# Moving small jobs of ScalarE, VectorE and TensorE by one weight chunk, and writing a loop of merge rounds out

## The reference

```python
# first block
mem_n = rms_norm(mem, norm_mem_g);  h = rms_norm(x, norm_in_g)
proj = h @ w_in                      # qa, ka, va, za, qb, kb, vb, zb, qm, zm, gates
ya = moba_attention(rope(qa), rope(ka), va) * silu(za)      # 8 heads of 128, causal here
yb = dilated_mixture(rope(qb), rope(kb), vb) * silu(zb)     # 3 groups of 4 heads
ym = memory_attention(qm, mk, mv) * silu(zm)                # mk, mv = mem_n @ w_mem_kv
merged = g_a * (ya @ w_proj_a) + g_b * (yb @ w_proj_b) + g_m * (ym @ w_proj_m)
x = rms_norm(x + merged @ w_out)
# second block
u = rmsnorm(x);  proj = u @ w_in_2   # lru_x, lru_g, q, k, v, ret_g
y = concat(rg_lru(conv(lru_x)) * gelu(lru_g), retention(rope(q), rope(k), v) * silu(ret_g))
h = x + y @ w_out_2
u = rmsnorm(h);  h = h + (silu(u @ w_gate) * (u @ w_up)) @ w_down
out = rmsnorm(h)
```

## Time and profile before

| | |
|---|---|
| runs | 2203.16, 2203.64, 2203.76 us (median 2203.64) |
| profiled execution: span | 2202.4 us |
| profiled execution's own time | not recorded apart; its span and what lies around it |
| granted TensorE clock | full speed, 0.99 and more in every slice |
| TensorE busy | 2185.7 us, 99% |
| VectorE busy | 1308.7 us, 59% |
| ScalarE busy | 1025.3 us, 47% |
| weight loads, SP's queue | 408.7 MB, 59.9% of the 16 DMA engines |
| carries, POOL's queue | 53.5 MB, 8.0% |

### The profile page before, as it was taken

One profiled execution on the slowest core, in us unless ns is written; L12 is line 12 of the kernel. 1 busy time (PEld: TensorE's weight loads), 2 busy tenths in 40 slices (PEclk: granted clock), 3 DMA queues, 4 the chain that ended last, 5 costly groups with the idle time before them and its releaser, 6 DMA issues.

```text
span 2202.4 us, 26200 instructions
## 1 busy us (share of the span) xinstructions
PE 2185.7 (99%) x9906; PEld 1811.4 (82%) x9906; DVE 1308.7 (59%) x1646; ACT 1025.3 (47%) x1235; POOL 144.2 (7%) x242
## 2 busy tenths in 40 slices
PE   9999999999999999999999999999999999999998
PEld 7888888887888888888888888888888888888886
DVE  5655656666455645546676878665555555554454
ACT  5544444443444444444554666454444444444443
POOL 0010101011000000000111100110001000100000
PEclk9999999999999999999999999999999999999999
DMA  8775656567754657667778756586777777776664
GB/s 293 219 230 177 203 164 214 182 225 220 219 163 148 211 177 229 201 204 282 228 259 249 229 182 200 192 247 210 211 211 225 220 211 211 227 236 193 194 194 146
DMA packets 228673, 464.65 MB, mean 211 GB/s; under 512 B 16344, under 2 KB 16608, under 8 KB 227680
## 3 DMA queue, kind: packets, MB, share of 16 engines
q1 hardware_dynamic: 212128, 408.73, 59.9%
q0 software_dynamic: 15712, 53.49, 8.0%
q10 hardware_dynamic: 736, 1.12, 0.1%
HBM read 437.59 MB, written 25.69 MB: 210 GB/s over the span
## 4 chain that ended last, share of the span: by engine, by line
PE 90%; DVE 4%; DMA 3%; ACT 1%; issue 1%; POOL 0%; POOLq 0%; ACTq 0%; DVEq 0%
PE ps L1485 29%; PE ps L1487 29%; PE ps L1486 29%; DVE w_lo L861 1%; DMA stage<-bounce 1%; PE ps L1345 1%; ACT w_hi L575 1%; PE ps L1376 1%; PE ps L1398 1%; DMA bounce<-tmp 1%; DVE tmp L1023 1%; DVE tmp L1014 0%; DVE stage L1009 0%; DVE stage L1018 0%; DMA raw<-in_w_out 0%
## 5 line engine op out<-in xcount | busy, mean ns | idle before, releaser
L861 DVE TENSOR_TENSOR w_lo<-raw,w_hi 128x1024 fp32r<-128x1024 f32 (+1 forms) x776 | 931.5, 1211 | 766.8 <-ACT w_hi L575 764.9
L575 ACT ACTIVATE w_hi<-raw 128x1024 fp32r<-128x1024 f32 (+1 forms) x776 | 810.3, 1050 | 917.2 <-PE ps L1487 824.5
L1485 PE MATMUL ps<-w_hi,xT_hi 128*128 128x512 f32 x1088 | 430.2, 395 | 1.6 <-DVE w_lo L861 1.6
L1487 PE MATMUL ps<-w_hi,xT_lo 128*128 128x512 f32 x1088 | 424.2, 390 | 0.0
L1486 PE MATMUL ps<-w_lo,xT_hi 128*128 128x512 f32 x1088 | 423.6, 389 | 0.0
L1485 PE MATMUL ps<-w_hi,u2T_hi 128*128 128x512 f32 x704 | 274.0, 389 | 0.0
L1487 PE MATMUL ps<-w_hi,u2T_lo 128*128 128x512 f32 x704 | 273.9, 389 | 0.0
L1486 PE MATMUL ps<-w_lo,u2T_hi 128*128 128x512 f32 x704 | 273.9, 389 | 0.0
L1485 PEld LDWEIGHTS ps<-w_hi,xT_hi 128*128 128x128 f32 x1088 | 204.4, 188 | 44.1 <-DVE w_lo L861 3.3
L1487 PEld LDWEIGHTS ps<-w_hi,xT_lo 128*128 128x128 f32 x1088 | 204.2, 188 | 43.5
L1486 PEld LDWEIGHTS ps<-w_lo,xT_hi 128*128 128x128 f32 x1088 | 204.5, 188 | 40.7
(11 more groups left out here) (262 smaller groups left out, 2259.3 us busy)
## 6 DMA issues: line engine op xcount, KB each, us to landing
raw<-in_w_in SPq DMA_DIRECT2D x368, 512.0 KB, 4.5
raw<-in_w_ffn_gate SPq DMA_DIRECT2D x88, 512.0 KB, 4.3
raw<-in_w_ffn_up SPq DMA_DIRECT2D x88, 512.0 KB, 4.5
raw<-in_w_ffn_down SPq DMA_DIRECT2D x88, 512.0 KB, 4.0
raw<-in_w_out SPq DMA_DIRECT2D x64, 512.0 KB, 5.1
bounce<-tmp POOLq DMA_DIRECT2D x41, 512.0 KB, 3.3
stage<-bounce POOLq DMA_DIRECT2D x164, 128.0 KB, 5.3
raw<-in_w_mem_kv SPq DMA_DIRECT2D x32, 512.0 KB, 5.7
```

What stands on the lines that cost most here:

```text
L575: nc.scalar.activation(w_hi[:, s, 0:per], raw[:, s, 0:per], ACT.Copy).then_inc(hi_ready, 1)
L861: nc.vector.tensor_tensor(w_lo[:, s, 0:per], raw[:, s, 0:per], w_hi[:, s, 0:per].bitcast(F32), ALU.subtract)\
L1485: nc.tensor.matmul(bank(2 * par + t), x_hi, w_hi[:, s, k], start=first, stop=False)
L1487: ins = nc.tensor.matmul(bank(2 * par + t), x_lo, w_hi[:, s, k], start=False, stop=last)
```

## The change

Six edits, all of order:

1. Mem's squares: two Squares behind split 6 become one behind split 6 and one behind split 7; VectorE's `mem_factors` goes from behind split 7 to behind split 1 of the next tile.
2. Units 5, 6 and 9, 10, 11 get `y_late`: TensorE turns y after chunk 6 instead of 5, and `unit_hi` and `unit_lo` go from the end of the tile to behind split 1 of the next one.
3. The six rotary blocks of qb and kb are marked "late", so that `use_late` stands behind split 3 where it stood behind split 1. For qb nothing changes, since blocks posted in a unit's tile are already late.
4. The residual's `post` on VectorE goes from behind split 3 to behind split 4 in w_out's tiles, ScalarE's `post_job` for bounced residuals from 4 to 5.
5. `ret_decay(4)` goes from chunk 4 to chunk 3 of the tail.
6. `w.rounds` for the merge rounds is replaced by a Python loop on SP, ScalarE, VectorE and TensorE: the same work in straight code.

```diff
@@ -334,13 +334,15 @@
                         dict(w=w_in, col=c + 3072, x="x", post=("silu", za[half][:, :, :]))]
                 for n in range(4):
                     four[n]["unit"] = mem_unit(n) if half == 0 else moba_unit(n)
+                    four[n]["y_late"] = half == 1 and n in (1, 2)
                 out_ += four
-            ten = [dict(w=w_in, col=QB + NW * g, x="x", post=("rope", qbT, g * QUAD)) for g in range(3)]
-            ten += [dict(w=w_in, col=KB + NW * g, x="x", post=("rope", kbT, g * QUAD)) for g in range(3)]
+            ten = [dict(w=w_in, col=QB + NW * g, x="x", post=("rope", qbT, g * QUAD, "late")) for g in range(3)]
+            ten += [dict(w=w_in, col=KB + NW * g, x="x", post=("rope", kbT, g * QUAD, "late")) for g in range(3)]
             ten += [dict(w=w_in, col=VB + NW * g, x="x", post=("take", vb[:, g])) for g in range(3)]
             ten += [dict(w=w_in, col=ZB, x="x", post=("silu", zb[:, :, :]))]
             for n in range(4):
                 ten[n]["unit"] = moba_unit(QUAD + n)
+                ten[n]["y_late"] = n > 0
             return out_ + ten
 
         def tiles_merge(n, first=False):
@@ -473,7 +475,8 @@
             load(second, {h: lambda h=h: load_x(h // QUAD, h % QUAD) for h in range(NT * QUAD)})
             sp.dma_start(consts[:, C_ID + P:], consts_d[:, C_ID + P:]).then_inc(in_tables, 16)
             load_all(rest + tiles_attention() + tiles_merge(0))
-            w.rounds(sp, NG - 1, lambda i: load_all(tiles_merge(i + 1)))
+            for i in range(NG - 1):
+                load_all(tiles_merge(i + 1))
             w.rounds(sp, NG // 2, lambda i: load_all(res_tiles(w_out, "m", None, i)))
             load_all(tiles_two())
             load_all(tiles_out2())
@@ -575,14 +578,18 @@
                 nc.scalar.activation(w_hi[:, s, 0:per], raw[:, s, 0:per], ACT.Copy).then_inc(hi_ready, 1)
                 w.step("g")
 
+            def square(src, sums, t):
+
+                if w.n["sq"]:
+                    act.wait_ge(sq_done, w.n["sq"])
+                nc.scalar.activation(sq_out[:, 0:D], src[:, t], ACT.Square, accum_out=sums[:, t:t + 1]).then_inc(sq_done, 1)
+                w.step("sq")
+
             def squares(src, sums, ready):
 
                 for t in range(NT):
                     ready(t)
-                    if w.n["sq"]:
-                        act.wait_ge(sq_done, w.n["sq"])
-                    nc.scalar.activation(sq_out[:, 0:D], src[:, t], ACT.Square, accum_out=sums[:, t:t + 1]).then_inc(sq_done, 1)
-                    w.step("sq")
+                    square(src, sums, t)
 
             def tile_squares(prev):
 
@@ -733,6 +740,8 @@
                 unit = tile.get("unit")
                 for h, _ in enumerate(chunks(tile)):
                     split(tile)
+                    if prev and prev.get("y_late") and h == 1:
+                        unit_hi(prev["unit"])
                     if h == late_in(tile, late):
                         use_late()
                     if "lru" in tile and h == 1:
@@ -749,11 +758,11 @@
                         lru_tanh(tile["lru"])
                     if "lru" in tile and h == 6:
                         lru_sqrt(tile["lru"])
-                    if h == pos(tile, 7 if unit else 4 if prev and prev["post"][0] == "res" and bounced(prev["post"]) else 6):
+                    if h == pos(tile, 7 if unit else 5 if prev and prev["post"][0] == "res" and bounced(prev["post"]) else 6):
                         post_job(prev, bool(unit))
                     for f in dict(hooks).get(h, ()):
                         f()
-                if unit and unit_chunk(tile, h) == 7:
+                if unit and unit_chunk(tile, h) == 7 and not tile.get("y_late"):
                     unit_hi(unit)
                 if "lru" in tile:
                     lru_hi(tile["lru"])
@@ -779,7 +788,7 @@
 
             four = tiles_memkv()
             four[0]["act_hooks"] = {1: jobs(memT_hi, V_MEM, 1), 3: jobs(memT_hi, V_MEM, 2), 5: jobs(memT_hi, V_MEM, 3),
-                                    6: [mem_in, lambda: squares(mem_tok, sumsq_m, lambda t: None)]}
+                                    6: [mem_in, lambda: square(mem_tok, sumsq_m, 0)], 7: [lambda: square(mem_tok, sumsq_m, 1)]}
             four[1]["act_hooks"] = {7: [lambda: act.wait_ge(b_out, 16),
                                         lambda: squares(x_tok, sumsq_x, lambda t: act.wait_ge(in_x[t], 16 * QUAD))]}
             for n in (2, 3):
@@ -810,7 +819,8 @@
             tiles[0]["act_hooks"] = {1: last}
             prev = chain(tiles, prev)
             prev = chain(tiles_merge(0, first=True), prev)
-            w.rounds(act, NG - 1, lambda i: chain(tiles_merge(i + 1), merge_last(i)))
+            for i in range(NG - 1):
+                chain(tiles_merge(i + 1), merge_last(i))
             prev = merge_last(NG - 1, "end")
             for k in range(NG // 2):
                 prev = chain(res_tiles(w_out, "m", x1, k, what="u"), prev)
@@ -1157,6 +1167,8 @@
                 unit = tile.get("unit")
                 for h, _ in enumerate(chunks(tile)):
                     split(tile)
+                    if prev and prev.get("y_late") and h == 1:
+                        unit_lo(prev["unit"])
                     if h == late_in(tile, late):
                         use_late()
                     if "lru" in tile and h == 2:
@@ -1165,7 +1177,7 @@
                         ret_lo(prev["ret"])
                     if unit and unit_chunk(tile, h) == 4:
                         unit_mask(unit)
-                    if h == pos(tile, 5 if unit else 3):
+                    if h == pos(tile, 5 if unit else 4 if prev and prev["post"][0] == "res" and bounced(prev["post"]) and prev["post"][3] == "u" else 3):
                         post(prev, h + 1)
                     if "ret" in tile and h == 4:
                         ret_decay(tile["ret"])
@@ -1177,7 +1189,8 @@
                         f()
                 if unit and unit_chunk(tile, h) == 7:
                     unit_norm(unit)
-                    unit_lo(unit)
+                    if not tile.get("y_late"):
+                        unit_lo(unit)
                 if "lru" in tile:
                     lru_scan(tile["lru"])
                 if "ret" in tile:
@@ -1275,7 +1288,8 @@
                 w.step("j0", "h0")
 
             four[0]["dve_hooks"] = {0: [second_half], 1: jobs(memT_hi, memT_lo, V_MEM, 1), 3: jobs(memT_hi, memT_lo, V_MEM, 2),
-                                    5: jobs(memT_hi, memT_lo, V_MEM, 3), 7: [mem_factors]}
+                                    5: jobs(memT_hi, memT_lo, V_MEM, 3)}
+            four[1]["dve_hooks"] = {1: [mem_factors]}
             for n in (2, 3):
                 four[n]["dve_hooks"] = {6: jobs(xT_hi, xT_lo, V_IN, 2 * n - 4), 7: jobs(xT_hi, xT_lo, V_IN, 2 * n - 3)}
             last = four[3]["dve_hooks"].pop(7)
@@ -1287,7 +1301,8 @@
             tiles[0]["dve_hooks"] = {1: last}
             prev = chain(tiles, prev)
             prev = chain(tiles_merge(0, first=True), prev)
-            w.rounds(dve, NG - 1, lambda i: chain(tiles_merge(i + 1), merge_last(i)))
+            for i in range(NG - 1):
+                chain(tiles_merge(i + 1), merge_last(i))
             prev = merge_last(NG - 1, "end")
             for k in range(NG // 2):
                 tiles = res_tiles(w_out, "m", x1, k, what="u")
@@ -1302,7 +1317,7 @@
             first_half = dict(tiles[4])
             tiles[6]["dve_hooks"] = {1: [lambda: turn_rows(h2, slice(0, NW))], 3: [lambda: post_job(first_half, False)]}
             tail_hooks(tiles[:6], "dve_hooks", {
-                4: [lambda: ret_decay(4)], 5: [lambda: ret_norm(4)],
+                3: [lambda: ret_decay(4)], 5: [lambda: ret_norm(4)],
                 7: [lambda: ret_decay(5), lambda: ret_lo(4)], 8: [lambda: ret_norm(5)],
                 10: [lambda: ret_decay(6), lambda: ret_lo(5)], 11: [lambda: ret_norm(6)],
                 13: [lambda: ret_decay(7), lambda: ret_lo(6)], 14: [lambda: ret_norm(7), lambda: ret_lo(7), lambda: dve.wait_ge(in_h2, 16 * NT * NG)],
@@ -1466,7 +1481,7 @@
                 unit, need, hooks = tile.get("unit"), tile.get("need", {}), tile.get("pe_hooks", {})
                 if w.n[f"a{par}"]:
                     pe.wait_ge(acc_free[par], w(f"a{par}"))
-                at_ = (0, 2, 4, 5)
+                at_ = (0, 2, 4, 6 if tile.get("y_late") else 5)
                 by_rows = SLOTS if tile.get("by_rows") else 0
                 for i, h in enumerate(chunks(tile)[:hcs - by_rows]):
                     s = w.n["g"] % SLOTS
@@ -1578,7 +1593,8 @@
             for k, units in ((3, 4), (4, 12), (5, 16)):
                 tiles[k]["need"] = {0: [lambda units=units: pe.wait_ge(u_lo, units)]}
             prev = chain(tiles, prev)
-            w.rounds(pe, NG - 1, lambda i: chain(tiles_merge(i + 1), merge_last(i)))
+            for i in range(NG - 1):
+                chain(tiles_merge(i + 1), merge_last(i))
```

## The result

| | before | changed |
|---|---|---|
| median of 9 runs, us | 2203.16 | 2207.91 |
| lowest to highest, us | 2201.0 to 2204.03 | 2205.89 to 2211.07 |
| span of the profiled execution, us | 2202.4 | 2205.0 |
| that execution's own time, us | not recorded apart | 2206.8 |

The ratio is 1.0021, 95% interval 1.0013 to 1.0030: by the medians the change costs 4.75 us. Forecast were 2202.8 and a range up to 2206.4, so the result lies outside it, on the side of the slower rival. All ratios in this document leave out two executions far above the others at a lower clock, one of e6 (4124 us) and one of the kernel before that was run beside e5 to e8 (3149 us).

The account below looks back on a forecast made before the run. TensorE, almost always busy, was taken as the bound, with only its stalls winnable. Gains of 4.8 and 1.05 against 5 d at d = 1.0 netted 0.8 us: 2202.8 us from the median, range 2198.2 to 2206.4.

Parts of the forecast that it names:

- the slower rival: Turns of units 7, 10, 11 and chunk 164: carries slowed by 2.1 us each, time 2208.2 us; chance 0.08.
- The five small edits: Squares, rotary copies, merge rounds, residual posts and retention's decay: gains of 4.77 us together from removed TensorE stalls.
- the squares: Mem's squares, stall at chunk 7: gain 0.69 us, or nothing if chunk 8 then stalls instead.
- the two rotary places: Chunk 4 after a rotary carry: moving the copy behind split 3 gains 0.64 + 1.06 = 1.70 us.
- the rounds: First chunks of the looped merge rounds: written out, they gain 0.12 + 0.40 + 0.11 = 0.63 us.
- the residual: Stall at 1092.17: the post behind chunk 4's w_lo gains 0.94 us; a later carry may return up to 0.9.
- the retention: Stall at 1386.09: decay one chunk earlier gains 0.81 us, or nothing if the scores it reads were late.
- The ends of the units: Five y stalls, 2.05 us, go with y later; waits at unit 7's turn and chunk 164 leave 1.05 net.
- The loop: Units' closed chain of turn, transpose, bounce, stage, copy, split, mask, exp: limits units once y does not; carry delays add up.
- d: Slowing of each stage carry 7 to 11 by earlier weight loads: 1.0 us, bounds 0.2 and 2.1, counted five times.
- the rival: Merge rounds: writing them out does nothing, VectorE being late for another reason; 0.6 missing, 2203.4 us; no separate chance given.
- The rule of turns between the queues: Stage carries: DMA engines alternate queues by packet, so a load 1.9 us sooner takes half; estimated d 0.9, sum -1.3.

Follow-up runs that it names:

- e6: Changed kernel with the loads of chunk 4 held until yT_lo is written and the rotary copy behind the exp in units' tiles; 2198.45 us, ratio 0.9980.
- e5: Changed kernel without y_late and with the rotary copy behind the exp in units' tiles; 2200.84 us, ratio 0.9988.
- e8: Changed kernel with y_late on units 6 and 10 alone, which are not neighbours; 2203.21 us, ratio 1.0001.
- e3: Changed kernel, but SP holds the load of chunk 4 behind each y_late unit until VectorE has written its yT_lo; 2197.28 us, ratio 0.9968.
- e4: Changed kernel with the rotary carry's copy behind the exp in units' tiles, not ahead of split 4; 2199.91 us, ratio 0.9982.
- e7: Changed kernel with only the load of chunk 5 behind each y_late unit held until yT_lo is written, chunk 4's left early; 2205.59 us, ratio 1.0009.
- e9: Changed kernel with the load of chunk 4 behind each y_late unit waiting for one w_lo more; 2203.09 us, ratio 1.0001.
- e2: Kernel before the change with y_late alone added; 2214.18 us, ratio 1.0052.
- e1: Changed kernel with y_late taken out and the other five edits kept; 2198.65 us, ratio 0.9982.

## Why the prediction was wrong

**The five small edits**: right in sign and place, all of them, and the sum a little too small: 4.77 by the brackets, and 5.5 came. By the offsets between the passes of both kernels the squares gave 0.9 (0.69 forecast), the two rotary places 0.5 and 1.4 (0.64 and 1.06), the rounds 0.7 (0.63), the residual 1.1 (0.94) and the retention 0.9 (0.81). At the squares and the second rotary place some 0.15 of it comes a few passes behind the stall, which the bracket does not show. Nothing came back at chunk 5 of the residual tiles.

**The ends of the units**: the y stalls went, as said, and the turns of units 7, 10 and 11 and chunk 164 took their place, as said; that of unit 6 too, which I had not named. The loop was right, e3 and e4 break it at two links. That its delays add up from unit to unit is shown only in part, by e8. The y stalls gave back 3.0 us where I had 2.05.

**The step that failed is the size of d.** I read 7.2 us now and 8.3 with the first load 0.6 us behind, put between two single carries, and rounded to 1.0. Measured is 8.80 - 7.13 = 1.67, and over all profiled executions with the first load about 2.5 or 0.5 us behind, e6 and e7 left out, some 2.2 (6.85 and 9.10). The row at 1.6 us (7.4) on which the interpolation hung is one carry, and e9's five at 1.7 average 7.8, from 7.0 to 8.6; a single carry's spread was as large as the effect. With 1.67, -5.8 + 5 x 1.67 = +2.5, close to the 2.6 by which the profiled span grew, though by luck, since two errors cancel: 0.9 us more gained outside the units (0.2 of it at the start, by no edit), and 1.0 more lost in them (8.3 against 7.3).

**The step that was missing is the clock.** I priced a stall at its own length. The one at turn 7 grew to 3.4 us, since the carry's slip met the smallest slack, and 1.6 us of slow passes came on top, in the changed kernel, in e2 and in e7. (I had worked out the slip per carry and never the length of the single stall.)

**The range** reached to d = 1.7 and so held the 1.67 of this profile by a hair. What it did not hold is the step from the profile to the median: I took the median at 1.2 us above the span, as before, and it lies 2.9 above it (2207.91 and 2205.0). Without these 1.7 us the result would stand at 2206.2, inside the range, with the cost of each carry wrong all the same. Part of this is that the changed kernel's runs spread over 5 us and the profiled one is a quick one. Why they spread more than the 3 us of before was not tried by itself; e9 spreads 9 us with as little slack, e1 3 us, and part of any spread can be the start, where the profiled executions alone differ by 3 us.

**The rivals.** The slower one was the right mechanism in the right places, at a chance of 0.08, which was too low: its threshold, d of 1.9, left out the clock. Its time, 2208.2, was all but met, yet with a d of 1.67 and not 2.1, so by luck. The rounds did bring all of 0.63, so the rival falls: the entry and the exit of the loop, which the rule on taken branches (Trainium skill, Runtime: NRT & Kernel Launch, "Instruction fetch mechanics") leaves as they are, went from 0.39 and 0.38 to 0.27 too, so the rule would explain 0.40 of it and the trace shows the rest; no run parts the branch from the loop's register work. The rule of turns between the queues (Trainium skill, DMA: Bandwidth & Descriptors, "Queues, rings and completion order") gave 0.9 by an even split, an estimate; the profile after has 1.67 for 2 us, e7 1.5, and e9 0.7 for 0.8 us. The sign agrees, the size is well over the even split; why was not tried.

## What to carry to other kernels

A job that is moved away from a queue's head lets through what stood behind it, and that may be a release of a buffer and with it a DMA: before moving it, look at which transfer will start sooner and what is in flight then. Here the move cost 8 us, and one wait on the queue that issues the loads took that away; e3, the changed kernel with that wait, is 0.9968 [0.9956, 0.9981] of before and beats both. Most of this gain is that of the five other edits: without `y_late` at all (e1) it is 0.9982 [0.9973, 0.9991], and the two intervals overlap, so that the late y is a gain by itself, 1.4 us by the medians and 2.4 by the profiles, is likely and not shown. Where a closed loop of engines and DMAs runs beside the bounding engine with 0.3 us of slack, price anything that touches its transfers by several of them, not by one.

## What the runs showed that I had not expected

- A load that starts 0.5 us behind the first of the four stage DMAs lengthens their landing by 1.5 us alone, and the second by only 0.2 more, less than the spread (e7). The four are issued over 2.4 us, and a load that starts behind the last costs little (e3).
- Nominally equal carries differ much: before, with the first load 2.5 us behind in four of five, they took 6.55 to 7.85 us. A cost of 1 us can't be read from one of them.
- A stall of 3.40 and of 3.35 us (changed kernel, e2) was followed by some 3.6 us at 1.2 GHz, and the wait of 2.1 us at the start of e3 by passes at 1.2 GHz too; one of 3.44 us (e8) was followed by none. The length of the stall alone does not decide it. What does was not tried.
